# An mLSTM projection that works on the un-normalised residual, with the norm's scale multiplied in where each product leaves PSUM

## The chip, the cores and the metric

One core of one Trainium2 chip runs the whole program in a single launch. The metric is the device time of one execution in microseconds (us). It is called the same within 0.2%, which is 1.6 us here.

## The reference

The reference takes 256 tokens of width 1024, puts 16 learned tokens in front (272 in all) and runs two blocks. What matters for this change is the first:

```
h = h + 0.5 * rmsnorm(swiglu(rmsnorm(h, g0)), g1)      # feed-forward 0, called f0 in the kernel
u = rmsnorm(h, g2)
y = mlstm_mixer(u)                                      # stage a
h = h + rmsnorm(y, g3)
h = h + 0.5 * rmsnorm(swiglu(rmsnorm(h, g4)), g5)      # feed-forward 1, f1

rmsnorm(x, g) = x * rsqrt(mean(x*x) + 1e-6) * g         # mean over the 1024 features of a token

mlstm_mixer(u): z = u @ w_in
    q, k = silu(causal_conv(z[qk columns], 4 taps)); v, og, gates = other columns of z
    lf = log_sigmoid(forget gates);  mLSTM over 8 heads;  y = h_out * sigmoid(og);  return y @ w_out
```

The second block has two layers (l0, l1): modulated norm, projections, attention and a short convolution, an output product and a post-norm added to the residual.

The scale of a norm is one number for each token. A product with weights is linear, so `(h * g2 * r) @ w` equals `r * ((h * g2) @ w)` when r belongs to the token.

## The kernel before

**Layout.** The residual `hT` lies transposed, features on the 128 partitions in 8 tiles of 128, tokens along the free axis (272 in f0 and a, 256 later). Every matrix product runs as three matmuls for each 128x128 weight tile, of the rounded weight `w1` and its remainder `w2` with the rounded activation `u1` and its remainder `u2` (`products`, L309). The weights come as 245 chunks of 128x1024 through five buffers. ScalarE rounds a chunk to `w1` (L739), VectorE makes `w2` (L1033), and five buffers of each are kept (NW = 5). So `split_to(c)` in either engine's program is the order to convert all chunks up to c at that place, and TensorE starts a block of 24 matmuls only when its chunk's `w2` is there.

**Order.** Each engine runs a written list of instructions in order. Engines meet at semaphores only. PSUM banks 0 to 3 are given out in rotation by `place` (L298), which waits until the bank's earlier content is read; banks 4 to 7 are named.

**Between f0 and a.** `normalised` (L1247) on VectorE computes from the column sums of f0's output the scale r1 of its own norm, then from three sums the scale r2 of the next norm (`first_scale` L1191, `second_scale` L1219). GpSimd takes both powers (L1603) and TensorE spreads each over the partitions with transposes (`spread` L369, `both_scales` L494), with `dense` filler matmuls between. Tile by tile VectorE then scales y (L1236), adds it to h for tiles 0 and 4 (GpSimd adds the others, L1609), multiplies h by gain and r2 into `tmp` (L1276), ScalarE rounds it (L841) and VectorE makes the remainder (L1255). TensorE's `head` (L334) takes three chunks at once (gates, qk 0, v 0) tile by tile as u arrives.

**Between a and f1** the kernel already works in the other way (`weighed` L1424): u is h times the gain alone, made before r2 is known. r2 is spread in the middle of the head and copied to `r0`, and the evacuation of the gate product multiplies by `r0`.

**Inside the mLSTM.** For j = 0 to 7 TensorE makes qk block j, v block j and the transposes of v block j-1 (L521). ScalarE's list for each j is: convert chunk A, copy the qk product to `zp` (L857), start the convolution in `cv` with the last tap (L858), convert chunk B, copy v to `vT` (L864), for j = 2 and 3 a part of the logarithm of the forget gate, and the silu of the finished convolution (L874). VectorE's list is: chunk A, three taps (L1346), chunk B, copy the transposed v to `Vs` (L1333), for j = 2, 4 and 5 steps of the gates (`log_gates`). Chunk A of j is chunk 70+2j+1, chunk B 70+2j+2. At j = 7 they are 85 and 86; before that, VectorE and ScalarE convert 70, and 71 to 73 at j = 1.

Then for heads h = 0 to 7: TensorE makes the output-gate block og h+2, transposes y h-1 (L564), sums over the keys (L556), and for each pair of heads makes mask and scores (L536, L545). VectorE adds the mask (L1366), ScalarE takes exponentials (L891), VectorE multiplies by the scores (L1377), makes denominators (L1384 to L1390) and gates the output (L1394), and ScalarE takes the tanh of og from PSUM (L883) and scales the numerators (L899, L900).

**At the end** `token_outputs` (L679) takes all four rotation banks ahead of its first product.

## Time and profile before

| what | us |
|---|---|
| median of 3 runs | 808.71 (808.56 to 810.04) |
| profiled execution, device time | 810.16 |
| its span | 808.2 |
| TensorE busy in the span | 798.9 (99%) |
| VectorE busy | 593.4 (73%) |
| ScalarE busy | 417.0 (52%) |
| GpSimd busy | 145.6 (18%) |
| granted TensorE clock, mean | 0.993 |

A busy share says how much of the span an engine worked, not whether the work was in time. TensorE is nearly always busy, so what counts is each place where it has to wait for the others, and how early the others are elsewhere. The 1.96 us between the span and the device time lie before and after the recorded instructions.

### The profile page before, as it was taken

The page shows a single profiled execution, that of the slowest core. Times are in us where ns is not written, and L with a number is a line of the kernel's source. Part 1 is how long each engine was busy: PE and PEld are TensorE (multiplying, and loading weights), DVE is VectorE, ACT ScalarE, POOL GpSimd, SP SyncE. Part 2 cuts the span into 40 slices and gives each one's busy share as a digit, 9 for nine tenths or more (in the row PEclk, how much of TensorE's full clock was granted, in tenths as well). Part 3 has the DMA queues.
Part 4 walks back from the last instruction along what each step waited for, and adds up shares of the span by engine and source line. Part 5 has one row for each costly group of instructions (what it writes and reads, how often), then busy time and mean ns, then how long its engine had stood idle before and what let it go on. Part 6 is the DMA issues. An engine that isn't in the chain of part 4 may idle for free.

```text
span 808.2 us, 15624 instructions
## 1 busy us (share of the span) xinstructions
PE 798.9 (99%) x6338; PEld 774.1 (96%) x6338; DVE 593.4 (73%) x957; ACT 417.0 (52%) x710; POOL 145.6 (18%) x158
## 2 busy tenths in 40 slices
PE   9999999999999999999999999999999999999997
PEld 9999999999999999999999999999899999899986
DVE  6777777698687986788777779986667567667653
ACT  7544444544367565555444455536655454565541
POOL 3800000041320000020000004240235302035510
PEclk9999999999899999999999999999999999999999
DMA  9876667685336643558777779546544651744531
GB/s 328 307 260 227 237 241 249 205 320 180 118 113 214 191 127 82 179 183 302 272 238 257 252 237 337 167 131 212 161 150 132 181 165 56 268 138 144 148 101 52
DMA packets 45190, 158.83 MB, mean 197 GB/s; under 512 B 5040, under 2 KB 6576, under 8 KB 45120
## 3 DMA queue, kind: packets, MB, share of 16 engines
q1 hardware_dynamic: 45120, 157.85, 58.9%
q8 instruction: 50, 0.82, 0.4%
q14 instruction: 20, 0.16, 0.1%
HBM read 156.76 MB, written 1.06 MB: 195 GB/s over the span
## 4 chain that ended last, share of the span: by engine, by line
PE 96%; DVE 2%; issue 1%; ACT 0%; POOL 0%; DVEq 0%; POOLq 0%
PE ps L312 26%; PE ps L314 25%; PE ps L313 25%; PE ps L664 3%; PE ps L357 2%; PE ps L353 2%; PE ps L354 2%; PE ps L365 1%; PE ps L328 1%; PE ps L556 1%; PE ps L628 1%; PE ps L647 1%; PE ps L637 1%; PE ps L690 1%; PE ps L692 1%
## 5 line engine op out<-in xcount | busy, mean ns | idle before, releaser
L1033 DVE TENSOR_TENSOR w<-raw,w 128x1024 fp32r<-128x1024 f32 x245 | 299.4, 1235 | 135.5 <-ACT w L739 135.1
L312 PE MATMUL ps<-u,w 128*128 128x256 f32 (+1 forms) x1231 | 353.2, 287 | 0.0
L314 PE MATMUL ps<-u,w 128*128 128x256 f32 (+1 forms) x1231 | 349.7, 284 | 0.0
L313 PE MATMUL ps<-u,w 128*128 128x256 f32 (+1 forms) x1231 | 349.0, 284 | 0.0
L739 ACT CAST w<-raw 128x1024 fp32r<-128x1024 f32 x245 | 254.1, 1049 | 124.4 <-PE ps L314 104.7
L312 PEld LDWEIGHTS ps<-u,w 128*128 128x128 f32 x1231 | 232.1, 189 | 6.2 <-issue 4.3
L314 PEld LDWEIGHTS ps<-u,w 128*128 128x128 f32 x1231 | 232.3, 189 | 0.0
L313 PEld LDWEIGHTS ps<-u,w 128*128 128x128 f32 x1231 | 231.6, 188 | 0.0
L312 PE MATMUL ps<-h,w 128*128 128x272 f32 (+1 forms) x352 | 100.3, 285 | 0.0
L314 PE MATMUL ps<-h,w 128*128 128x272 f32 (+1 forms) x352 | 100.0, 284 | 0.0
L313 PE MATMUL ps<-h,w 128*128 128x272 f32 (+1 forms) x352 | 99.8, 284 | 0.0
L1594 POOL TENSOR_TENSOR sqa<-sqa,sq 128x272 f32<-128x272 f32 (+1 forms) x12 | 15.7, 1308 | 311.1 <-ACT sq L804 311.1
L312 PEld LDWEIGHTS ps<-h,w 128*128 128x128 f32 x352 | 66.3, 188 | 0.0
L313 PEld LDWEIGHTS ps<-h,w 128*128 128x128 f32 x352 | 66.2, 188 | 0.0
L314 PEld LDWEIGHTS ps<-h,w 128*128 128x128 f32 x352 | 66.1, 188 | 0.0
L1624 POOL TENSOR_SCALAR Sb<-Sb,st 128x256 f32<-128x256 f32 x32 | 45.2, 1428 | 87.9 <-DVE st L1473 87.9
L1052 DVE SCALAR_TENSOR_TENSOR acc<-adr,cact,acc 128x1024 f32<-128x1024 f32 x42 | 58.2, 1406 | 0.0
L782 ACT ACTIVATE si<-tmp 128x272 f32<-128x272 f32 (+1 forms) x44 | 18.7, 424 | 70.3 <-DVE tmp L1145 70.3
L1150 DVE TENSOR_TENSOR hf<-si,ps 128x272 f32<-128x272 f32 (+1 forms) x44 | 18.9, 429 | 21.2 <-ACT si L782 21.2
L1603 POOL TENSOR_TENSOR rst<-sst,eps 128x2 f32<-128x2 f32 (+1 forms) x4 | 3.0, 748 | 148.8 <-DVE sst L1196 135.5
L353 PE MATMUL ps<-u,w 128*128 128x256 f32 (+1 forms) x105 | 27.2, 290 | 1.2 <-ACT u L926 0.8
L354 PE MATMUL ps<-u,w 128*128 128x256 f32 (+1 forms) x105 | 26.8, 286 | 0.0
(252 smaller groups left out, 1045.2 us busy)
## 6 DMA issues: line engine op xcount, KB each, us to landing
raw<-wst SPq DMA_DIRECT2D x245, 512.0 KB, 4.6
adr<-wada SPq DMA_DIRECT2D x48, 512.0 KB, 3.9
Bt<-bias_rows SPq DMA_DIRECT2D x8, 192.0 KB, 4.0
hT<-xT SPq DMA_DIRECT2D x4, 272.0 KB, 5.2
outT<-yg SPq DMA_DIRECT2D x4, 256.0 KB, 2.0
cs<-cst SPq DMA_DIRECT2D x1, 140.0 KB, 5.1
cs<-cst SPq DMA_DIRECT2D x1, 128.0 KB, 7.0
vc<-vec SPq DMA_DIRECT2D x1, 101.0 KB, 3.5
```

Of the source, the lines that this page charges most:

```text
L312: e.matmul(out, a, x1, start=first, stop=False)
L313: e.matmul(out, a, x2, start=False, stop=False)
L314: return e.matmul(out, b, x1, start=False, stop=last)
L353: e.matmul(ps[:, b, 0:n], w1[:, (c + j) % NW, o:o + P], x1[:, kt, :], start=i == 0, stop=False)
L354: e.matmul(ps[:, b, 0:n], w2[:, (c + j) % NW, o:o + P], x1[:, kt, :], start=False, stop=False)
L664: m = e.matmul(ps[:, b_[tt], :], xx[:, kt, 128 * tt:128 * tt + 128], ww, start=kt == 0 and i == 0, stop=kt == 7 and i == 2)
L739: e.copy(w1[:, k % NW, :], raw[:, k % NRAW, :]).then_inc(*tick(s_upper, k))
L782: e.activation(si[f][:, j % 2, :], zg[:, j % 2, 0:n], ACT.Silu).then_inc(*tick(s_si, (f, j)))
L1033: e.tensor_tensor(w2[:, k % NW, :], raw[:, k % NRAW, :], w1[:, k % NW, :].bitcast(F32), ALU.subtract).then_inc(*tick(s_split, k))
L1052: e.scalar_tensor_tensor(a, w, x, a, ALU.mult, ALU.add).then_inc(*tick(s_acc, k))
L1150: e.tensor_tensor(hf[f][:, i, :], si[f][:, i, :], out_of(ku, n), ALU.mult).then_inc(*reading(ku))
L1624: e.tensor_scalar(Sb[l][:, h % 4, t, :], Sb[l][:, h % 4, t, :], st_[l][:, h % 4, 4 + t:5 + t], None, ALU.mult).then_inc(*tick(s_nrm, (l, h ...
```

## The change

1. **f0 to a** goes the way of a to f1. `weighed` takes the stage as an argument on ScalarE and VectorE, TensorE's `both_scales("f0", T)` is gone, 4 dense matmuls and the spread of r1 stand at the start of its `mlstm`, and the spread of r2 is a hook in the middle of the head. u is h times gain 2.
2. **r2 at the evacuations.** VectorE multiplies each qk product (8 of 128x272), the two gate products (8x272) and each og product (8 of 128x256) by `r0` on the way out of PSUM. ScalarE's copy to `zp` is gone; its first tap and its tanh read SBUF now, after VectorE. `v` is scaled after its transposes: `r0` is transposed once (3 transposes on TensorE, two small copies to `rv` on VectorE), and ScalarE copies V to `Vs` with three multiplies by a column of `rv` for each head, where VectorE copied it with two copies.
3. **Fewer norm steps**, at every boundary: the sums are read from PSUM by `tensor_scalar` with two column operands, without the copies and the separate add.
4. **Last banks one by one**: `token_outputs` takes a bank ahead of the first product that writes it.
5. GpSimd adds h tile 2 between the two powers in f0 too, and leaves tile 1 to VectorE. Its clears of `Vs` and `SW` wait for the spread of r1 in place of that of r2, and for the clear of `zp`, which VectorE now does after it has copied `r0`. One more memset (`msq`) stands at the start.

```diff
             def mlstm():                                             # TensorE
+                dense(4)
+                e.wait_ge(s_pow.handle, at(s_pow, ("r1", "f0")))
+                spread(("r1", "f0"), 6, T, rst)
+                def spread_scale(i):
+                    if i == KT // 2:
+                        e.wait_ge(s_pow.handle, at(s_pow, ("r2", "f0")))
+                        spread(("r2", "f0"), 5, T, rst2)
+                def scale_columns():
+                    b = place(("rv",), 6)
+                    e.wait_ge(*read(("r2", "f0")))
+                    for j, (a, z) in enumerate(tok_tiles(T)):
+                        m = e.transpose(ps[0:z - a, b, 128 * j:128 * j + 128], r0[:, a:z], ident)
+                    m.then_inc(*tick(s_rvtr, 0))
...
-                head(keys[:3], c, x1, x2, T, *u_of("a"))
+                head(keys[:3], c, x1, x2, T, *u_of("a"), hook=spread_scale)
                 for j in range(8):
                     if j:
                         block(("qk", j), c + 1 + 2 * j, x1, x2, T)
+                        if j == 1:
+                            scale_columns()
...
             def token_outputs():
-                b_ = [[place(("tok", t, hf)) for hf in range(2)] for t in range(2)]
...
-                        out = ps[:, b_[t][hf], :]
+                        out = ps[:, place(("tok", t, hf)) if i == 0 else bank_of(("tok", t, hf)), :]
...
             ffn_out(0, "f0", T)
-            both_scales("f0", T)
             mlstm()
...
             def mlstm():                                             # ScalarE
-                e.wait_ge(s_zero.handle, 1)
+                def v_scaled(h):
+                    b = bank_of(("vt", h))
+                    e.wait_ge(s_vtr.handle, at(s_vtr, h))
+                    if h == 0:
+                        e.wait_ge(s_pad.handle, at(s_pad, "last"))
+                        e.wait_ge(*read(("rv",)))
+                    for j, n in enumerate((P, P, NMETA)):
+                        m = e.mul(Vs[0:n, j, h, 0:128], ps[0:n, b, 128 * j:128 * j + 128], rv[0:n, j:j + 1])
+                    m.then_inc(*reading(("vt", h)))
                 split_to(c + NW - 1)
                 for j in range(8):
                     if j:
                         split_to(c + 1 + 2 * j + NW - 1)
-                    proj(("qk", j))
-                    if j > 1:
-                        e.wait_ge(s_cv.handle, at(s_cv, (j - 2, 2)))
-                    e.copy(zp[:, i, 3:3 + T], out_of(("qk", j), T)).then_inc(*tick(s_zp, j))
-                    e.mul(cv[:, i, :], out_of(("qk", j), T), a_tap(3, j)).then_inc(*reading(("qk", j)))
+                    e.wait_ge(*read(("qk", j)))
+                    e.mul(cv[:, i, :], zp[:, i, 3:3 + T], a_tap(3, j)).then_inc(*tick(s_cvm, j))
                     if j:
                         split_to(c + 2 + 2 * j + NW - 1)
                     proj(("v", j))
...
                     e.copy(vT[:, i, :], out_of(("v", j), T)).then_inc(*reading(("v", j)))
+                    if j:
+                        v_scaled(j - 1)
...
                 def gate_block(h):
                     split_to(c + 17 + h + NW - 1)
-                    proj(("og", h))
-                    e.activation(og[:, h, :], out_of(("og", h)), ACT.Tanh, scale=0.5).then_inc(*reading(("og", h)))
+                    e.wait_ge(*read(("og", h)))
+                    e.activation(og[:, h, :], og[:, h, :], ACT.Tanh, scale=0.5).then_inc(*tick(s_tanh, ("og", h)))
...
                 gate_block(1)
+                v_scaled(7)
...
             def first_scale(s, n, eps_of):                           # VectorE: sst, then
+                e.reciprocal(inv[:, 0:len(tt)], sst[:, 0:len(tt)]).then_inc(*tick(s_stat, ("inv", s)))
+                e.wait_ge(s_stat.handle, at(s_stat, ("inv", s)))
+                for j, (a, z) in enumerate(tt):
+                    m = e.tensor_scalar(msq[0:z - a, j:j + 1], ps[0:z - a, 7, 2 * j + 1:2 * j + 2], inv[0:z - a, j:j + 1],
+                                        msh[0:z - a, j:j + 1], ALU.mult, ALU.add)
...
             def second_scale(s, n):
+                for j, (a, z) in enumerate(tt):
+                    m = e.tensor_scalar(msq[0:z - a, j:j + 1], ps[0:z - a, 5, j:j + 1], rst[0:z - a, j:j + 1],
+                                        msq[0:z - a, j:j + 1], ALU.mult, ALU.add)
+                e.tensor_scalar(msh[:, 0:len(tt)], msq[:, 0:len(tt)], EPS, None, ALU.max).then_inc(*tick(s_stat, ("max", s)))
...
             def mlstm():                                             # VectorE
-                e.wait_ge(s_spread.handle, at(s_spread, ("r2", "f0")))
                 e.memset(zp[:, :, 0:3], 0.0).then_inc(*tick(s_zero, 0))
-                split_to(c + NW - 1)
                 proj(("gates",))
+                e.wait_ge(*read(("r2", "f0")))
-                e.tensor_scalar(gi, ps[0:8, b, 0:T], vc[0:8, V_GB:V_GB + 1], None, ALU.add).then_inc(*tick(s_gate, "i"))
-                e.tensor_copy(fx_, ps[32:40, b, 0:T]).then_inc(*reading(("gates",)))
+                e.tensor_tensor(gi, ps[0:8, b, 0:T], r0[0:8, :], ALU.mult).then_inc(*tick(s_gate, "zi"))
+                e.tensor_tensor(fx_, ps[32:40, b, 0:T], r0[32:40, :], ALU.mult).then_inc(*reading(("gates",)))
+                e.wait_ge(s_gate.handle, at(s_gate, "zi"))
+                e.tensor_scalar(gi, gi, vc[0:8, V_GB:V_GB + 1], None, ALU.add).then_inc(*tick(s_gate, "i"))
...
                 for j in range(8):
                     if j:
                         split_to(c + 1 + 2 * j + NW - 1)
-                    e.wait_ge(s_zp.handle, at(s_zp, j))
+                    proj(("qk", j))
+                    if j > 1:
+                        e.wait_ge(s_cv.handle, at(s_cv, (j - 2, 2)))
+                    e.tensor_tensor(zp[:, i, 3:3 + T], out_of(("qk", j), T), r0, ALU.mult).then_inc(*reading(("qk", j)))
+                    if j == 1:
+                        e.wait_ge(s_rvtr.handle, 1)
+                        e.tensor_copy(rv[:, 0:2], ps[:, 6, 0:256:128])
+                        e.tensor_copy(rv[0:16, 2:3], ps[0:16, 6, 256:257]).then_inc(*reading(("rv",)))
                     for tap in range(3):
                         if tap == 0:
-                            e.wait_ge(*read(("qk", j)))
+                            e.wait_ge(s_cvm.handle, at(s_cvm, j))
...
                     if j:
                         split_to(c + 2 + 2 * j + NW - 1)
-                        v_copied(j - 1)
...
+                def gate_scaled(h):
+                    proj(("og", h))
+                    e.tensor_tensor(og[:, h, :], out_of(("og", h)), r0[:, 16:T], ALU.mult).then_inc(*reading(("og", h)))
                 split_to(c + 17 + NW - 1)
+                gate_scaled(0)
                 weights(0)
                 weighted(0)
                 split_to(c + 18 + NW - 1)
-                v_copied(7)
+                gate_scaled(1)
                 for h in range(NH):
                     if h < NH - 2:
                         split_to(c + 19 + h + NW - 1)
+                        gate_scaled(h + 2)
...
-            normalised("f0", "a", T, lambda k: norm_gain(2, k), None, eps0)
+            weighed("f0", "a", T, 2, C_A, eps0)
```

In `weighed` VectorE's list is that of a to f1: first scale; tile by tile scaled y, h added (tiles 0, 1, 4), the remainder of u; the second scale after tile 1; then chunk C_A + 4 = 70 and the copy to `r0`.

## Rows read from the trace of the kernel before

**Rows 1.** The page's chain that ended last, share of the span by engine.
```profile
PE 96%; DVE 2%; issue 1%; ACT 0%; POOL 0%; DVEq 0%; POOLq 0%
```
**Rows 2.** Windows: length, busy us of PE, PEld, DVE, ACT, POOL; clock; DMA; GB/s.
```profile
213.80:220.60 6.80, 6.80 (x31) 6.04 (x31) 5.25 (x16) 1.26 (x3) 3.31 (x5) 0.50 0.10 34
```
**Rows 3.** Timeline of PE, f0 to a: start, us, instruction, [idle before <- releaser].
```profile
214.94 1.65 PE L328 MATMUL ps<-dz 128*128 128x256 f32 x6
...
218.61 0.43 PE L353 MATMUL ps<-u,w 128*128 128x272 f32 x1
```
**Rows 4.** Timeline of DVE: chunks 79, 81 and 83, and the first pair's weights.
```profile
255.79 1.23 DVE L1033 TENSOR_TENSOR w<-raw,w 128x1024 fp32r<-128x1024 f32 x1 [3.85 <-ACT w L739]
256.93 1.57 DVE L1346 SCALAR_TENSOR_TENSOR cv<-zp,vc,cv 128x272 f32<-128x272 f32 x3
...
262.68 1.19 DVE L1033 TENSOR_TENSOR w<-raw,w 128x1024 fp32r<-128x1024 f32 x1
...
269.74 1.21 DVE L1033 TENSOR_TENSOR w<-raw,w 128x1024 fp32r<-128x1024 f32 x1
...
280.88 1.33 DVE L1366 TENSOR_TENSOR SW<-ps,cs 128x256 f32<-128x256 f32 x6
282.73 1.53 DVE L1377 SCALAR_TENSOR_TENSOR SW<-ps,SW 128x256 f32<-128x256 f32 x6 [0.53 <-ACT SW L891]
```
**Rows 5.** Timeline of PE: sums over the keys of heads 0, 2 and 4.
```profile
285.06 1.28 PE L556 MATMUL ps<-Vs,SW 128*128 128x129 f32 x10
...
294.85 1.28 PE L556 MATMUL ps<-Vs,SW 128*128 128x129 f32 x10
...
304.63 1.28 PE L556 MATMUL ps<-Vs,SW 128*128 128x129 f32 x10
```
**Rows 6.** Timeline of DVE: mask added for pairs 1, 2 and 3.
```profile
287.76 1.31 DVE L1366 TENSOR_TENSOR SW<-ps,cs 128x256 f32<-128x256 f32 x6
...
297.28 1.33 DVE L1366 TENSOR_TENSOR SW<-ps,cs 128x256 f32<-128x256 f32 x6
...
307.16 1.33 DVE L1366 TENSOR_TENSOR SW<-ps,cs 128x256 f32<-128x256 f32 x6
```
**Rows 7.** Timeline of PE: last matmul before, first matmul of the token outputs.
```profile
777.59 0.28 PE L314 MATMUL ps<-u,w 128*128 128x256 f32 x1
...
779.17 0.47 PE L690 MATMUL ps<-w,m 128*128 128x512 f32 x1 [1.31 <-DVE cw L1521]
```
**Rows 8.** Timeline of DVE and ACT, a to f1.
```profile
343.11 0.42 DVE L1236 TENSOR_TENSOR yg<-yg,ps 128x256 f32<-128x256 f32 x1 [0.65 <-PE ps L372]
...
353.03 0.51 ACT L926 ACTIVATE u<-hT,vc 128x256 fp32r<-128x256 f32 x1 [1.17 <-POOL hT L1609]
```
**Rows 9.** Timeline of ACT in the mLSTM, the part of j = 3.
```profile
246.49 1.03 ACT L739 CAST w<-raw 128x1024 fp32r<-128x1024 f32 x1
...
247.71 0.48 ACT L858 ACTIVATE cv<-ps,vc 128x272 f32<-128x272 f32 x1
248.09 1.04 ACT L739 CAST w<-raw 128x1024 fp32r<-128x1024 f32 x1
249.03 0.37 ACT L864 COPY vT<-ps 128x272 f32<-128x272 f32 x1
249.42 1.28 ACT L870 ACT_TABLE_LOAD   x1
...
254.29 0.53 ACT L874 ACTIVATE qk<-cv,vc 128x272 f32<-128x272 f32 x1
254.72 1.03 ACT L739 CAST w<-raw 128x1024 fp32r<-128x1024 f32 x1
```
**Rows 10.** Timeline of ACT: numerators of head 1 scaled.
```profile
293.42 0.37 ACT L899 ACTIVATE ytm<-ps,den 128x128 f32<-128x128 f32 x1
293.68 0.36 ACT L900 ACTIVATE ytm<-ps,den 128x128 f32<-128x128 f32 x1
```
**Rows 11.** Timeline of POOL, l0 to l1: the second power.
```profile
671.17 0.71 POOL L1603 TENSOR_TENSOR rst<-msh,eps 128x2 f32<-128x2 f32 x1 [0.72 <-DVE msh L1233]
```

More of the change, by code:

```diff
@@ L1191, in first_scale @@
             def first_scale(s, n, eps_of):
-                nt = len(sum_tiles(n))
+                tt = sum_tiles(n)
                 e.wait_ge(s_colsum.handle, at(s_colsum, ("sum", s) if s[0] == "f" else ("sq", s, 7)))
                 if eps_of is None:
-                    e.tensor_scalar(sst[:, 0:2], ps[:, 7, 0:4:2], EPS, None, ALU.add).then_inc(*tick(s_stat, ("sst", s)))
+                    m = e.tensor_scalar(sst[:, 0:2], ps[:, 7, 0:4:2], EPS, None, ALU.add)
                 else:
                     m = e.tensor_tensor(sst[:, 0:2], ps[:, 7, 0:4:2], eps_of[:, 0:2], ALU.add)
-                    if nt == 3:
+                    if n == T:
@@ L1216, in first_scale @@
-                e.wait_ge(s_stat.handle, at(s_stat, ("quot", s)))
-                e.tensor_tensor(msh[:, 0:nt], msh[:, 0:nt], inv[:, 0:nt], ALU.add).then_inc(*tick(s_stat, ("msh", s)))
-            def second_scale(s, n):
-                nt = len(sum_tiles(n))
-                e.wait_ge(s_stat.handle, at(s_stat, ("msh", s)))
-                e.wait_ge(s_pow.handle, at(s_pow, ("r1", s)))
-                if nt == 3:
-                    e.wait_ge(*read(("sumc", s)))
-                    e.tensor_tensor(inv[:, 0:nt], sums[:, 6:9], rst[:, 0:nt], ALU.mult).then_inc(*tick(s_stat, ("mix", s)))
-                    e.wait_ge(s_stat.handle, at(s_stat, ("mix", s)))
-                else:
-                    e.wait_ge(s_colsum.handle, at(s_colsum, ("sumc", s)))
-                    e.tensor_tensor(inv[:, 0:nt], ps[:, 5, 0:2], rst[:, 0:nt], ALU.mult).then_inc(*reading(("sumc", s)))
-                    e.wait_ge(*read(("sumc", s)))
-                e.tensor_tensor(msh[:, 0:nt], msh[:, 0:nt], inv[:, 0:nt], ALU.add).then_inc(*tick(s_stat, ("add", s)))
-                e.wait_ge(s_stat.handle, at(s_stat, ("add", s)))
-                e.tensor_scalar(msh[:, 0:nt], msh[:, 0:nt], EPS, None, ALU.max).then_inc(*tick(s_stat, ("max", s)))
@@ L1422, in mlstm, with weighed @@
                 mixer_out("a", c + 25)
-            def weighed():
-                first_scale("a", S, None)
-                e.wait_ge(s_spread.handle, at(s_spread, ("r1", "a")))
-                e.wait_ge(*read(("out", "a", KT - 1)))
+            def weighed(s, nxt, n, g, c, eps_of):
+                first_scale(s, n, eps_of)
+                e.wait_ge(s_spread.handle, at(s_spread, ("r1", s)))
+                e.wait_ge(*read(("out", s, KT - 1)))
                 for k in range(-1, KT):
                     if k < KT - 1:
-                        scaled("a", k + 1, S)
+                        scaled(s, k + 1, n)
@@ L1443, in weighed @@
-                split_to(C_F[1] + NW - 1)
-                e.wait_ge(s_spread.handle, at(s_spread, ("r2", "a")))
-                e.tensor_copy(r0[:, 0:S], ps[:, 5, 0:S]).then_inc(*reading(("r2", "a")))
+                        second_scale(s, n)
+                        if s == "a":
+                            e.wait_ge(s_stat.handle, at(s_stat, ("max", "a")))
+                            e.tensor_scalar(eps0[:, 0:2], msh[:, 0:2], EPS, None, ALU.mult).then_inc(
+                                *tick(s_stat, ("eps", "a")))
@@ L1447, in attention @@
+                split_to(c + NW - 1)
+                e.wait_ge(s_spread.handle, at(s_spread, ("r2", s)))
+                if s == "a":
+                    e.wait_ge(*read(("og", NH - 1)))
+                e.tensor_copy(r0[:, 0:n], ps[:, 5, 0:n]).then_inc(*reading(("r2", s)))
             def attention(l):
@@ L1569, in first_input @@
                 e.memset(sst[:, :], 1.0).then_inc(*tick(s_one, "sst"))
+                e.memset(msq[:, :], 1.0).then_inc(*tick(s_one, "msq"))
                 e.wait_ge(s_one.handle, at(s_one, "sst"))
@@ L1611, in boundary @@
             def boundary(s, n):
-                nt = len(sum_tiles(n))
-                e.wait_ge(s_stat.handle, at(s_stat, ("sst", s)))
-                power(rst, sst, nt, ("r1", s))
-                e.wait_ge(s_stat.handle, at(s_stat, ("max", s)))
-                power(rst2, msh, nt, ("r2", s))
+                first_power(s, n)
+                second_power(s, n)
                 h_added(s, n, (1, 2, 3, 5, 6, 7))
```

82 lines of the change are left out of this document (39 added, 43 removed).

## The prediction

> **What bounds the kernel now.** I read the page's chain first, then the granted clock around the change, then each engine's timeline there, and asked at each place how early the other engines are. The chain is 96% TensorE [rows 1], so a gain must come from a place where TensorE waits or runs slowly, and a loss from an engine that is only just in time now. There are three such places.
>
> At f0 to a the array ran at half its clock (0.50 of 2.4 GHz, so the 1.2 GHz level) for 6.8 us [rows 2], after 24 matmuls of one or two columns, and six filler matmuls took 1.65 us there [rows 3]. The head began at 218.61 [rows 3]. The reader is to see that this stretch is short work at a low clock, where the order of the norm steps decides.
>
> In the mLSTM TensorE has no wait at all, but VectorE and ScalarE are hardly ahead of it. The mask of the first pair of heads is added at 280.88, the products with the scores end at 284.26 (282.73 + 1.53) [rows 4], and TensorE starts the sums that need them at 285.06 [rows 5]: 0.8 us of slack. Later the mask steps are 9.52 and 9.88 us apart [rows 6], where TensorE's sums are 9.79 and 9.78 apart [rows 5]. So the loop of VectorE and ScalarE is as long as TensorE's own. That the waits of TensorE are zero hides this.
>
> At the token outputs TensorE waits 1.31 us for a bank [rows 7].
>
> **The change part by part.** I sum against the profiled execution (span 808.2, 810.16 with what lies around it). It lies 1.45 above the median of 808.71, so the difference is applied to the median.
>
> *f0 to a, the start.* The first spread ends at about 215.0, just ahead of the fillers [rows 3]. Four fillers now stand ahead of it: 4 x 0.24 (1.65 less the overlap of the last, over 6) [rows 3] = 1.0, so it ends at 216.0. From the first scaled tile to the start of the last u the same code takes 9.92 us between a and f1 (343.11 to 353.03) and the last u takes 0.51 [rows 8]. I add 0.2 for 272 columns in place of 256 and take off 0.3 for the norm steps that are gone: the last u is there at 216.0 + 10.3 = 226.3. The first u comes 1.6 after the first scaled tile, so the head starts at 217.6, 1.0 earlier than 218.61 [rows 3], and it is no longer short of u tiles, which I put at 0.2 more. Extra on TensorE are the 3 transposes of the scale, 0.3. So TensorE gains 0.9 here, with bounds of 0.3 less (the fillers cost what they cost) and 1.4 more (the clock back at 217 and not at 220.6).
>
> *The chain of VectorE and ScalarE, entering the mLSTM.* It does not gain as much. From 226.3: cast of chunk 70 1.03, its remainder 1.23, the copy to r0 0.35, the gates' two products and bias 1.1, the product into zp 0.43 (as the scaling of y [rows 8]), first tap 0.5, three taps 1.57 [rows 4], silu 0.43. The waits between engines (0.04 each) and the overlap of successive instructions cancel to 0.1. The cast of chunk 71 then starts at 233.0, 0.4 earlier than before.
>
> *The loop over j.* Here the order changes. Before, ScalarE went cast A, zp, first tap, cast B, v, silu, while VectorE made the remainder of A: nothing that ScalarE did waited for VectorE but the silu. Now ScalarE's first tap waits until VectorE has made the remainder of A and then zp. ScalarE's round is cast A 1.03 [rows 9], wait for the remainder 1.18 (255.79 to 256.93, plus 0.04) [rows 4], wait for zp 0.47, first tap 0.39 (247.71 to 248.09), cast B 0.94 (248.09 to 249.03), v 0.28, three scalings of V 0.78, silu 0.43 (254.29 to 254.72) [rows 9]: 5.5 us, against 4.3 before (remainder A 1.14, taps 1.48, remainder B 1.14, V copies 0.53, all VectorE). The three scalings are priced by the numerators, 0.26 from start to start for 128x128 [rows 10]; their bounds are 0 (hidden beside the taps) and 1.1 (3 x 0.37). TensorE's round is 6.4, so the longer round alone would be covered. But two things take the cover: ScalarE's logarithm at j = 3 with three table loads (249.42 to 254.29) [rows 9], which stands behind the scalings, and VectorE's gate steps at j = 4 and 5, with which it was busy without a gap from 255.79 on (6.89 to chunk 81, 7.06 to chunk 83) [rows 4].
>
> Lateness of VectorE against before, chunk by chunk: -0.4 at 71. Chunk 75 +0.9: in j = 1 ScalarE has the scalings (0.8) and the taps stand behind zp (0.5). Chunk 77 +1.3. Chunk 79 +3.4: j = 3 waits for remainder and zp (1.6 less the 0.3 of the old copy) and has the scalings (0.8) ahead of the table loads. Then VectorE's own round is the bound: it gains zp and the wait for the first tap (1.0) and loses the V copies (0.5), +0.5 at each j, so chunk 81 +3.9 and 83 +4.4. At j = 6 and 7 ScalarE's 5.5 is the bound against 4.3: chunk 85 +5.6, 87 +6.8. The og product adds 0.35 ahead of the first mask: +7.2, at 288.1. The pair's products then end 3.38 later (280.88 to 284.26) [rows 4], at 291.5, and TensorE's sums start there and not at 285.06 [rows 5]: +6.4. On the way TensorE waits at the transposes of v 4 to 7 and for og 0, but these waits lie inside the 6.4.
>
> *The loop over heads.* First pair to second: 6.88 before (280.88 to 287.76) [rows 4, 6]. Now two og products (0.7), and head 7's scalings and the tanh stand ahead of a cast, where the V copies stood beside it: 9.3, +2.4, so the second mask is 9.6 late. After that each pair has two og products more on a loop that is serial through both engines (mask, exponentials, cast, remainder, og product, output, denominator, numerators, cast, and again): +0.65 for each of two pairs against 9.52 and 9.88 [rows 6], 10.3 and 10.9 late, and og 7 makes 11.2. At 10.5 a pair the loop is longer than TensorE's 9.78 [rows 5], so TensorE waits. It had about 1.0 of slack to the last outputs. So it enters a's output product 10.2 late. This holds the gain at f0 to a, which is lost: TensorE's early start only lengthens its wait.
>
> Bounds of this term: 6.4 if the loop over heads is hidden, 12 if the scalings cost 1.1 and every handover 0.1. The nearest rows give 10.2.
>
> *The end.* The bank of the first token product was read long before, that of the fourth is needed nine matmuls later. 779.17 - 777.59 - 0.12 of a normal step = 1.46 [rows 7], all of it gained, since TensorE alone is the bound to the end.
>
> *Fewer norm steps.* Into l0 and f1 a filler or the head covers them: nothing. Into l1 the second power starts at 671.17, 0.72 after GpSimd was free [rows 11], and one step of 0.1 less lies ahead of it: 0.1 gained, between 0 and 0.3. The extra memset and the moved clears cost nothing: the first V copy comes several us after them.
>
> *Sum.* +10.2 - 1.46 - 0.1 = +8.6; 808.7 + 8.6 = 817.3.
>
> **The rivals.** *All hidden, faster.* TensorE stays the bound through the mLSTM. For it speaks that TensorE shows no wait there and that its round over j, 6.4 us, is longer than ScalarE's new one; against it the 0.8 us of slack [rows 4, 5]. -0.9 - 1.46 - 0.1 = -2.5: 806.2, and 804.8 with the clock back sooner.
>
> *Only the loop over j costs.* The loop over heads catches up, if handovers there are shorter than I read. Against it are the 9.88 [rows 6]. +6.4 - 1.6 = +4.8: 813.5.
>
> *The clock falls in the new waits.* TensorE would wait some 1 to 2.5 us at six or more places, and it lost its clock at f0 to a after about 2.5 us of tiny matmuls [rows 2]. A stretch like that at half clock does 3.4 us less work, one of half its length 1.7. Where TensorE waits anyway it is free, so I count one such stretch that lies behind the loops or at their tight end: +1.7 to +3.4, 819 to 820.7. The Trainium skill (TensorE: Matmul & The Clock Gate, the section on HAM oscillation) says that waits between bursts of matmuls can put the array back to half its clock again and again. By that rule this rival is the likelier. The trace has the low level once more only, after f1, and not at a or l0, where waits of 0.2 to 0.8 us stand beside the sums, so I leave it behind the forecast.
>
> *The steps aren't fewer in time.* A `tensor_scalar` with two column operands may take longer than the copies: some 0.3 us at most at l1, in no way decisive.
>
> **How the numbers follow.** Forecast 0.59, 817.3, its own range 814.5 to 820. Loop over j only 0.13, 813.5. Clock 0.12, 820. All hidden 0.12, 806.2. The rest, 0.04, no change. The range 812.5 to 821 leaves out the hidden case and little else. What can be told from no change is 0.2%, 1.6 us: faster 0.13, same 0.03, slower 0.84.
>
> **What would show it.** Head of a starting about 1 us earlier; chunk 79's remainder near 259, chunk 87's near 286.6 and the first mask near 288; TensorE waiting for vT and later for the numerators and SW, some 10 us in all; mask steps 10.2 to 10.5 apart; no wait at L690. I am wrong if TensorE's waits between 228 and 322 stay under 2 us. Then the round of ScalarE is shorter than I add it up. A clock under 1.00 in the mLSTM would show the third rival.

## The result and the profile after

| what | before | after |
|---|---|---|
| median | 809.34 (4 runs beside those of after) | 821.55 (820.13 to 821.87, 4 runs) |
| ratio to before | | 1.0148, 95% interval 1.0132 to 1.0164 |
| profiled execution, its span | 810.16, 808.2 | 821.64, 819.6 |
| mean granted TensorE clock | 0.993 | 0.986 |

The changed kernel is slower by 12.2 us, 1.5%. The forecast was 817.3 with 812.5 to 821.0; the median lies 0.55 above the range.

The page's chain of after answers to [rows 1]:

```profile
PE 84%; DVE 7%; ACT 6%; issue 3%; POOL 1%; DVEq 0%; POOLq 0%; ACTq 0%
```

TensorE's share of the chain fell from 96% to 84%: 13% of it now runs through VectorE and ScalarE. TensorE's waits by releaser (us in total, times, longest) say where:

```profile
PE ps L543 <- ACT vT L889: 2.4, 2, 1.9
PE ps L582 <- ACT ytm L927: 2.2, 3, 1.5
PE ps L574 <- DVE SW L1394: 1.8, 1, 1.8
...
PE ps L314 <- DVE w L1061: 1.0, 1, 1.0
```

All four are in the mLSTM, where there was no wait before. They add up to 7.4 us. The wait for the token bank [rows 7] is gone: the first token product is L708 and starts without one.

```profile
790.66 0.40 PE L708 MATMUL ps<-w,m 128*128 128x512 f32 x1
```

VectorE as the mLSTM begins, from the copy of the scale to the first taps (timeline: start, us, instruction, [idle before <- releaser]):

```profile
228.49 0.43 DVE L1472 COPY tmp<-ps 128x272 f32<-128x272 f32 x1
...
229.03 0.43 DVE L1308 TENSOR_TENSOR g<-ps,tmp 8x272 f32<-8x272 f32 x1
229.49 0.43 DVE L1309 TENSOR_TENSOR g<-ps,tmp 8x272 f32<-8x272 f32 x1
229.96 0.64 DVE L1311 TENSOR_SCALAR g<-g,vc 8x272 f32<-8x272 f32 x1
230.63 0.44 DVE L1352 TENSOR_TENSOR zp<-ps,tmp 128x272 f32<-128x272 f32 x1
231.73 1.58 DVE L1364 SCALAR_TENSOR_TENSOR cv<-zp,vc,cv 128x272 f32<-128x272 f32 x3 [0.66 <-ACT cv L883]
```

The three gate steps stand in line ahead of zp and take 1.60 us (229.03 to 230.63). Then the round of j = 4 on VectorE, and the landmarks that answer to [rows 4, 6]:

```profile
260.09 1.23 DVE L1061 TENSOR_TENSOR w<-raw,w 128x1024 fp32r<-128x1024 f32 x1 [5.61 <-ACT w L756]
261.23 0.43 DVE L1352 TENSOR_TENSOR zp<-ps,tmp 128x272 f32<-128x272 f32 x1
262.25 1.58 DVE L1364 SCALAR_TENSOR_TENSOR cv<-zp,vc,cv 128x272 f32<-128x272 f32 x3 [0.59 <-ACT cv L883]
...
267.48 1.19 DVE L1061 TENSOR_TENSOR w<-raw,w 128x1024 fp32r<-128x1024 f32 x1
...
288.98 1.32 DVE L1383 TENSOR_TENSOR SW<-ps,cs 128x256 f32<-128x256 f32 x6
290.83 1.53 DVE L1394 SCALAR_TENSOR_TENSOR SW<-ps,SW 128x256 f32<-128x256 f32 x6 [0.53 <-ACT SW L918]
...
298.25 1.31 DVE L1383 TENSOR_TENSOR SW<-ps,cs 128x256 f32<-128x256 f32 x6
...
308.44 1.33 DVE L1383 TENSOR_TENSOR SW<-ps,cs 128x256 f32<-128x256 f32 x6
```

VectorE does zp, then idles 0.59 us until ScalarE has made the first tap from it. ScalarE on its side idles for zp: 1.64 us at j = 2, 3, 4 and 7, and 3.5 and 3.7 at j = 5 and 6, where VectorE has gate steps first. At j = 3:

```profile
248.53 1.03 ACT L756 CAST w<-raw 128x1024 fp32r<-128x1024 f32 x1
251.20 0.52 ACT L883 ACTIVATE cv<-zp,vc 128x272 f32<-128x272 f32 x1 [1.64 <-DVE zp L1352]
251.63 1.04 ACT L756 CAST w<-raw 128x1024 fp32r<-128x1024 f32 x1
252.58 0.37 ACT L889 COPY vT<-ps 128x272 f32<-128x272 f32 x1
252.85 0.85 ACT L874 ACTIVATE Vs<-ps,rv 128x128 f32<-128x128 f32 x3
253.72 1.28 ACT L897 ACT_TABLE_LOAD   x1
```

Each engine waits for the other once in a round, so the round is the sum of both parts. TensorE's sums over the keys of head 0 answer to [rows 5]:

```profile
291.59 2.29 PE L574 MATMUL ps<-Vs,SW 128*128 128x129 f32 x10 [1.84 <-DVE SW L1394]
```

Lateness of after against before, at the same instruction in both profiles, beside the forecast:

| point | before | after | late | forecast |
|---|---|---|---|---|
| VectorE, remainder of chunk 71 | 234.41 | 234.84 | +0.4 | -0.4 |
| chunk 79 | 255.79 | 260.09 | +4.3 | +3.4 |
| chunk 87 | 279.73 | 287.50 | +7.8 | +6.8 |
| first mask | 280.88 | 288.98 | +8.1 | +7.2 |
| masks of pairs 1, 2, 3 | | | +10.5, +11.2, +11.8 | +9.6, +10.3, +10.9 |
| TensorE, first low products of a's output | 314.33 | 325.44 | +11.1 | +10.2 |
| f1's head, second low products | 347.07 | 358.77 | +11.7 | +10.2 |
| f1's column sums | 528.12 | 540.31 | +12.2 | +10.2 |
| l0's column sums | 668.20 | 681.00 | +12.8 | +10.2 |
| l1's head, second low products | 675.95 | 688.81 | +12.9 | +10.1 |
| first token product | 779.17 | 790.66 | +11.5 | +8.6 |

Two things stand in it. From chunk 71 on to a's output the lateness runs parallel to the forecast, 0.8 to 1.0 above it. And behind a it grows by another 1.8 us, where the forecast had nothing. The experiments take these in turn.

One thing the table hides. The two executions were not level ahead of the change: TensorE reaches f0's last column sums at 211.39 in before and at 210.94 in after. Counted from there, after is 0.45 later at every point than the table says, so 1.3 above the forecast at chunk 71 and not 0.8.

### The profile page after: what moved, and what is told of

It is laid out like the page before. It is cut to its first block, busy times and chain, and to the rows that moved or that the text cites. A ratio compares the mean times of both kernels' runs of the same rounds, so it can differ in the third digit from the quotient of the medians.

```text
span 819.6 us, 15624 instructions
## 1 busy us (share of the span) xinstructions
PE 804.7 (98%) x6339; PEld 778.6 (95%) x6339; DVE 593.9 (72%) x949; ACT 422.1 (51%) x726; POOL 145.1 (18%) x158
## 3 DMA queue, kind: packets, MB, share of 16 engines
HBM read 156.76 MB, written 1.06 MB: 193 GB/s over the span
## 4 chain that ended last, share of the span: by engine, by line
PE 84%; DVE 7%; ACT 6%; issue 3%; POOL 1%; DVEq 0%; POOLq 0%; ACTq 0%
PE ps L314 23%; PE ps L316 22%; PE ps L315 22%; PE ps L684 3%; DVE w L1061 2%; ACT w L756 2%; PE ps L355 2%; PE ps L356 2%; PE ps L359 2%; PE ps L367 2%; PE ps L330 1%; PE ps L648 1%; PE ps L667 1%; ACT SW L918 1%; PE ps L657 1%
## 5 line engine op out<-in xcount | busy, mean ns | idle before, releaser
L314 PE MATMUL ps<-u,w 128*128 128x256 f32 (+1 forms) x1231 | 354.1, 288 | 1.0 <-DVE w L1061 1.0
L314 PEld LDWEIGHTS ps<-u,w 128*128 128x128 f32 x1231 | 232.9, 189 | 7.5 <-issue 4.3
L314 PE MATMUL ps<-h,w 128*128 128x272 f32 (+1 forms) x352 | 100.5, 286 | 0.0
L314 PEld LDWEIGHTS ps<-h,w 128*128 128x128 f32 x352 | 66.3, 188 | 0.0
```

The costliest lines, as they stand in the source:

```text
L314: e.matmul(out, a, x1, start=first, stop=False)
```

## Experiments

Ratios are to the kernel before, in runs on the same chip (its medians there: 809.89 for the first four, 810.03 for the next four, 810.29 for the two after, 809.58 for the last two).

### Which evacuation costs: one scale at a time

The changed kernel with q and k, V and the output gates left unscaled (b1_none), and with one of the three scaled (b2_qk, b3_v, b4_og); where it isn't scaled, the order of before stands on both engines. The scale is left out there, so none of the four computes the whole reference. The excerpts below are from ScalarE's list, the last one from VectorE's, where b1_none copies V.

```diff
-                    e.wait_ge(*read(("qk", j)))
-                    e.mul(cv[:, i, :], zp[:, i, 3:3 + T], a_tap(3, j)).then_inc(*tick(s_cvm, j))
+                    proj(("qk", j))
+                    if j > 1:
+                        e.wait_ge(s_cv.handle, at(s_cv, (j - 2, 2)))
+                    e.copy(zp[:, i, 3:3 + T], out_of(("qk", j), T)).then_inc(*tick(s_cvm, j))
+                    e.mul(cv[:, i, :], out_of(("qk", j), T), a_tap(3, j)).then_inc(*reading(("qk", j)))
...
-                    if j:
-                        v_scaled(j - 1)
...
-                    e.wait_ge(*read(("og", h)))
-                    e.activation(og[:, h, :], og[:, h, :], ACT.Tanh, scale=0.5).then_inc(*tick(s_tanh, ("og", h)))
+                    proj(("og", h))
+                    e.activation(og[:, h, :], out_of(("og", h)), ACT.Tanh, scale=0.5).then_inc(*reading(("og", h)))
...
+                        v_copied(j - 1)
```

> The changed kernel, but the qk, v and og products leave PSUM unscaled, by the instructions and in the order of the kernel before (so q, k, v and og lack the norm's scale; the gates have it). It keeps the new boundary f0 to a, the fewer norm steps and the banks one by one. My theory (the chain of VectorE and ScalarE in the mLSTM is what costs, and only the evacuations put it there): no wait of TensorE between 228 and 322 us, 2 to 3 us faster than before. Rival (the cost is at the boundary: the fillers, the low clock, the late r0): still 8 us or more slower than before. Rival (half and half): within 2 us of before.

> As b1_none, but with the scale in the qk evacuations: VectorE makes zp and ScalarE's first tap waits for it. v and og are unscaled. My theory: the round over j grows from 4.3 to 5.1 us, chunk 79 is some 2.5 us late, the first mask some 5 to 6.5 late, so 2 to 4 us slower than before. Rival (the three scalings of V make the round long, zp is hidden): faster than before by 1 to 2.5 us.

> As b1_none, but with the scale in the copies of V (three multiplies on ScalarE for each head; scale transposed on TensorE). qk and og are unscaled. My theory: alone they fit in ScalarE's waits for the taps, only j = 3 and head 7 pay, 1 to 2.5 us faster than before. Rival (ScalarE's extra 0.8 us a head is the cost): 3 us or more slower than before.

> As b1_none, but with the scale in the og evacuations: VectorE multiplies, ScalarE's tanh waits for it. qk and v are unscaled. My theory: each pair of heads is 0.65 us longer, on a loop that had about 1 us of slack in all: mask steps 10.2 and 10.5 us apart, within 1.5 us of before. Rival (the loop over heads was only long because it was entered late): mask steps stay at 9.5 and 9.9, 2 to 3 us faster than before.

| kernel | median | ratio | interval | first mask | steps between masks |
|---|---|---|---|---|---|
| b1_none | 808.44 | 0.9978 | 0.9969 to 0.9988 | 279.75 | 6.88, 9.52, 9.89 |
| b2_qk | 817.02 | 1.0081 | 1.0066 to 1.0096 | 288.69 | 6.87, 9.53, 9.89 |
| b3_v | 807.98 | 0.9974 | 0.9964 to 0.9983 | 279.89 | 7.19, 9.53, 9.87 |
| b4_og | 812.15 | 1.0027 | 1.0018 to 1.0037 | 280.21 | 9.06, 10.18, 10.53 |

Over b1_none, q and k cost 8.6 us, the output gates 3.7, V nothing; together 11.8, against 13.0 to 13.8 for the whole change over b1_none by the ratios. The masks name the mechanisms. The product into zp makes the first mask 8.9 us later and leaves the steps as they were. The og products leave the first mask and make all steps longer, by 2.2, 0.7 and 0.6. The steps agree with the forecast for og (+2.4 and +0.65 twice), but the time does not agree with what I expected of b4_og: within 1.5 us of before, and it is 2.2 slower by its ratio. For V theory and size agree (three scalings cost 0.76 each round on ScalarE, which had that much room). b1_none was to be 2 to 3 us faster than before and is 1.8. Of q and k alone I had expected 2 to 4 us more than before; it came to 6.6, and is most of the loss. In each round VectorE has zp (0.43) more and idles 0.59 until the tap is there, and in this kernel it keeps the V copies (0.5) that the whole change takes off it.

### The banks of the token outputs alone

```diff
-                b_ = [[place(("tok", t, hf)) for hf in range(2)] for t in range(2)]
...
-                        out = ps[:, b_[t][hf], :]
+                        out = ps[:, place(("tok", t, hf)) if i == 0 else bank_of(("tok", t, hf)), :]
```

> The kernel before with one part of the change alone: the banks of the token outputs are taken one by one. Theory: the 1.46 us at the first token product are gained and nothing else moves, 1.2 to 1.7 us faster than before, no wait at L690. Rival (the wait is handed on to the next bank or to m2): within 0.5 us of before.

807.23, ratio 0.9975 (0.9955 to 0.9995). From l1's second low products to the first token product it takes 101.72 us, 103.22 before: 1.50 gained, the forecast's 1.46. Of the kernels that compute the whole reference it has the lowest ratio, though the intervals of e1_pad and f3_all below touch its own. (Its profiled span, 805.0, is 3.2 us shorter than that of before. The other 1.7 don't come from the banks: it reaches f0's column sums 0.55 earlier, and takes 0.6 less from them to the end of a's head, with a shorter stretch of low clock, and 0.5 less at l0's head, where it has none.)

### The same change in another order

f1_zp puts VectorE's product into zp ahead of the remainder of the chunk:

```diff
-                    if j:
-                        split_to(c + 1 + 2 * j + NW - 1)
                     proj(("qk", j))
...
                     e.tensor_tensor(zp[:, i, 3:3 + T], out_of(("qk", j), T), r0, ALU.mult).then_inc(*reading(("qk", j)))
+                    if j:
+                        split_to(c + 1 + 2 * j + NW - 1)
```

> The changed kernel with one move: in each j VectorE makes the product into zp ahead of the remainder of chunk A, not behind it. Theory (ScalarE's first tap and VectorE's taps wait for each other there, 1.0 us a round): the first mask comes about 5 to 6 us earlier than in the changed kernel (282 to 284 against 288.98), the loop over heads keeps its cost, 2 to 4 us slower than before. Rival (the added work as such costs, VectorE and ScalarE are full): within 2 us of the changed kernel, 10 or more slower than before.

f2_zp_og, on top of it, issues the og product behind the masks of the next pair (even heads) or behind the denominators (odd heads), and ScalarE's tanh a round later, behind the next cast. VectorE's list, then ScalarE's:

```diff
-                        gate_scaled(h + 2)
                     if 0 < h < NH - 2:
                         output(h - 1)
                     denominators(h)
                     if h % 2 == 0 and h < NH - 2:
                         weights(h // 2 + 1)
+                        gate_scaled(h + 2)
                         weighted(h // 2 + 1)
+                    elif h < NH - 2:
+                        gate_scaled(h + 2)
...
                     if h < NH - 2:
-                        gate_block(h + 2)
+                        split_to(c + 19 + h + NW - 1)
+                    if h < NH - 1:
+                        gate_tanh(h + 1)
```

> As f1_zp, and in the loop over heads the og product of VectorE stands where it waited for ScalarE (behind the denominators of odd heads, between the two steps of the weights of even heads), and ScalarE's tanh comes one round later, behind a cast; head 7's scalings of V stand ahead of that cast. Theory: mask steps back at 9.6 to 9.9 us, 2 us or more faster than f1_zp, between 2 us faster and 1 slower than before. Rival (this loop is bound by the sum of work): no faster than f1_zp.

f3_all, on top of that, makes zp of block 0 before the gates' products:

```diff
+                proj(("qk", 0))
+                e.wait_ge(*read(("r2", "f0")))
+                e.tensor_tensor(zp[:, 0, 3:3 + T], out_of(("qk", 0), T), r0, ALU.mult).then_inc(*reading(("qk", 0)))
                 proj(("gates",))
-                e.wait_ge(*read(("r2", "f0")))
```

> As f2_zp_og, and VectorE makes zp of block 0 ahead of the two gate products. Theory: the chain enters the loop over j up to 1 us earlier, 0.2 to 1 us faster than f2_zp_og, 0.5 to 2.5 faster than before. Rival (TensorE is the bound again in f2_zp_og already): the same as f2_zp_og.

| kernel | median | ratio | interval | first mask | steps |
|---|---|---|---|---|---|
| f1_zp | 814.22 | 1.0051 | 1.0036 to 1.0066 | 282.54 | 9.28, 10.19, 10.55 |
| f2_zp_og | 810.76 | 1.0013 | 1.0002 to 1.0024 | 280.81 | 6.93, 9.52, 10.14 |
| f3_all | 809.55 | 0.9994 | 0.9984 to 1.0003 | 280.99 | 6.92, 9.52, 10.13 |

The order alone brings the changed kernel back to the time of the kernel before: 7 us with zp early, 3 with the og products off the chain, and 1.2 by the medians (1.5 by the ratios) with the entry. The profiles show 0.7 of the last step: TensorE's wait for the remainder of chunk 71 is 0.97 us in f2_zp_og and 0.23 in f3_all. The first mask is no earlier there, since f3_all's profile ran at the low clock for longer at f0 to a (213.7 to 220.5, against 215.3 to 218.7). VectorE's round in f1_zp shows no idle time ahead of the taps any more:

```profile
257.51 1.23 DVE L1061 TENSOR_TENSOR w<-raw,w 128x1024 fp32r<-128x1024 f32 x1 [3.78 <-ACT w L756]
258.65 1.57 DVE L1364 SCALAR_TENSOR_TENSOR cv<-zp,vc,cv 128x272 f32<-128x272 f32 x3
260.13 1.22 DVE L1061 TENSOR_TENSOR w<-raw,w 128x1024 fp32r<-128x1024 f32 x1
```

So nearly all of the loss is the place of the products in two engines' lists, not their work. What is left is about 1.3 us: f3_all has 0.9994, b1_none, with the same boundaries and banks but no scaling of q, k, V and og, 0.9978, and their intervals only just overlap. In f3_all's mLSTM TensorE still waits twice, and the last mask step is 10.13 against 9.89:

```profile
235.65 0.39 PE L314 MATMUL ps<-u,w 128*128 128x272 f32 x1 [0.23 <-DVE w L1063]
...
314.12 0.35 PE L355 MATMUL ps<-y,w 128*128 128x256 f32 x1 [0.56 <-DVE og L1429]
```

Even in this order the change brings nothing over the banks alone (0.9975).

### The low clock in the new waits

After's profile has the low level (0.50) behind two of the new waits and at the start of f1. Windows of after (length, busy PE, PEld, DVE, ACT, POOL; clock; DMA share; GB/s):

```profile
260.00:264.00 4.00, 2.08 (x17) 1.85 (x16) 3.25 (x6) 2.36 (x7) 0.00 (x0) 1.00 0.37 108
264.00:268.00 4.00, 4.00 (x22) 4.00 (x21) 3.89 (x7) 1.54 (x3) 0.00 (x0) 0.57 0.64 201
...
291.00:295.50 4.50, 3.91 (x20) 3.48 (x20) 2.80 (x8) 2.87 (x9) 0.00 (x0) 0.62 0.32 95
...
352.00:358.00 6.00, 5.71 (x34) 5.42 (x35) 4.66 (x16) 1.59 (x5) 1.64 (x3) 0.72 0.38 108
```

That is the third rival's sign. d1_keep puts filler matmuls into the three longest waits, into the bank that is placed there anyway (`keep(b, n)` issues n of 128x256; ahead of the transposes of v 3, the sums over the keys of head 0, the output of head 1):

```diff
+                    b = place(("vt", h), None if h >= NH - 2 else 4 + h % 2)
+                    if h == 3:
+                        keep(b, 15)
                     e.wait_ge(*read(("v", h)))
-                    b = place(("vt", h), None if h >= NH - 2 else 4 + h % 2)
...
+                    if h == 0:
+                        b = place(("num", h))
+                        keep(b, 15)
                     e.wait_ge(*read(("score", h)))
...
+                    b = place(("y", h), 6)
+                    if h == 1:
+                        keep(b, 12)
                     e.wait_ge(*read(("num", h)))
-                    b = place(("y", h), 6)
```

> The changed kernel with filler matmuls (128x256, results overwritten) in TensorE's three longest new waits of the mLSTM: 15 ahead of the transposes of v 3 (it waits 1.9 us there), 15 ahead of the sums over the keys of head 0 (1.8), 12 ahead of the output of head 1 (1.5), each a little shorter than the wait. Theory A, the two stretches at half clock behind these waits (264.4 to 267.8 and 291.6 to 295.0) are absorbed, since VectorE and ScalarE set the order there: the clock in the mLSTM goes to 1.00, first mask at 289, mask steps 9.3, 10.2 and 10.5 as before, and the time stays within 0.7 us of the changed kernel without fillers. Theory B, the low clock there is part of the excess over the forecast: 1.7 us less for one stretch, 3.4 for both, that is 818 to 820.

> The changed kernel once more, for the comparison with the fillers on the same chip: 820 to 822, 1.013 to 1.017 of the kernel before. If the low stretches differ from those of its first profile (0.50 at 213.4 to 220.2, then 264.4 to 267.8, 291.6 to 295.0, and half the clock lost behind f1 and l0), the two profiles together show what such a stretch costs where it comes and where it does not.

d1_keep: 821.27, 1.0136 (1.0119 to 1.0153). The changed kernel again: 821.61, 1.0139 (1.0124 to 1.0155). In d1_keep the clock stays at its 2.4 GHz level through the mLSTM, and the masks stand where they stood:

```profile
260.00:264.00 4.00, 3.81 (x31) 3.60 (x30) 3.34 (x6) 2.70 (x7) 0.00 (x0) 1.00 0.53 148
264.00:268.00 4.00, 4.00 (x34) 4.00 (x33) 3.89 (x7) 1.15 (x2) 0.00 (x0) 1.00 0.53 164
...
291.00:295.50 4.50, 4.44 (x40) 3.84 (x40) 2.42 (x7) 2.87 (x8) 0.00 (x0) 1.00 0.29 74
```

```profile
288.58 1.32 DVE L1395 TENSOR_TENSOR SW<-ps,cs 128x256 f32<-128x256 f32 x6
...
297.87 1.31 DVE L1395 TENSOR_TENSOR SW<-ps,cs 128x256 f32<-128x256 f32 x6
```

Steps 9.29, 10.19 and 10.54, as in after. The clock did fall there, and it cost nothing: TensorE had to wait for VectorE at the next stop in any case. From f0's column sums to a's first low output products it is 114.50 us in after, 114.26 in the second profile of after and 114.51 in d1_keep.

Nor does such a wait always bring the low clock. The second profile of after has the same two waits:

```profile
264.26 0.55 PE L543 MATMUL ps<-cs,vT 128*128 128x128 f32 x3 [1.90 <-ACT vT L889]
...
292.37 1.65 PE L574 MATMUL ps<-Vs,SW 128*128 128x129 f32 x10 [1.80 <-DVE SW L1394]
```

Behind the first the granted clock stays at 1.00, behind the second it is 0.50 from 293.3 to 300.2. f1_zp and b4_og, with waits up to 1.5 us, have no low stretch there. Behind a the low clock costs a little. The column sums of a to f1's second low products take 6.70 us in before and 6.71 in the second profile of after, both at full clock, and 7.35 in the first profile, with the low stretch: 0.65. The same from l0 to l1 is 7.81 at full clock and 8.64 in the second profile, which has its low stretch there. The two profiles of after have their low stretches at different boundaries (the first at f1 and l0, the second at l1), and their spans, 819.6 and 820.1, are close.

### The missing microsecond: where the operands lie

Stage lengths on TensorE fall into two groups: before and a1_banks on one side, every kernel made from the changed one on the other. Within a group f1 is the same to 0.01 us (181.05; 181.53 to 181.54), l0 to 0.2 (127.41 to 127.44; 127.78 to 127.98). The changed one allocates two small buffers, msq and rv, 16 bytes a partition each, in the middle of the list, and all buffers behind them move by 16 to 32 bytes. e1_pad is a1_banks with such a gap and no other difference; e2_place is the changed kernel without it.

The gap of e1_pad, on a1_banks:

```diff
         msh = sb("msh", [P, 4])
+        pad1 = sb("pad1", [P, 4])
         rst2 = sb("rst2", [P, 4])
+        pad2 = sb("pad2", [P, 4])
```

e2_place, on the changed kernel, whose sums buffer has these columns free (its memset is narrowed to columns 0 to 7):

```diff
-        msq = sb("msq", [P, 4])
+        msq = sums[:, 8:12]
...
-        rv = sb("rv", [P, 4])
+        rv = sums[:, 4:8]
```

> The kernel before with the token banks one by one, and two unused buffers of 16 bytes a partition where the change allocates msq and rv, so that every buffer behind them lies where it lies in the changed kernel; no instruction differs. Stage lengths by TensorE in the profiles so far are the same to 0.02 us in each group of kernels and differ between the groups with and without the change's two buffers: f1 from its second low product to the column sums 181.05 without, 181.54 with; l0 likewise 127.4 without, 127.8 with; a's output product with its sums 26.04 without, 25.71 with; from l1's head to the first token product 101.72 without, 101.85 with. Theory A, where the operands lie sets this: 181.54, 127.8, 25.7 and 101.85 here, 0.6 to 0.8 us in all, so 807.8 to 808.2. Theory B, it is the fewer norm steps or their instructions: all four as without the change, and 807.2.

> The changed kernel with msq and rv laid into columns of the sums buffer that it no longer uses, so that every later buffer lies where it lies in the kernel before; the instructions are the same. Theory A (place of the operands): f1 181.05 in place of 181.54, l0 127.4 in place of 127.8, head of l1 to first token product 101.72; 0.6 to 0.9 us faster than the changed kernel, 820.5 to 821.0. Theory B: no stage changes, 821.5.

| stage on TensorE | before | a1_banks | e1_pad | after | e2_place |
|---|---|---|---|---|---|
| a, first low output products to column sums | 26.04 | 26.04 | 25.71 | (waits) | (waits) |
| f1, second low products to column sums | 181.05 | 181.05 | 181.54 | 181.54 | 181.05 |
| l0, the same | 127.44 | 127.41 | 127.80 | 127.79 | 127.31 |
| l1's second low products to first token product | 103.22 | 101.72 | 101.86 | 101.85 | 101.73 |

The ends of the f1 stage and of the l0 stage in a1_banks, and in e1_pad:

```profile
345.95 0.63 PE L357 MATMUL ps<-u,w 128*128 128x256 f32 x4
...
527.00 0.50 PE L365 MATMUL ps<-wts,sqa 128*128 128x1 f32 x4
...
539.14 0.63 PE L357 MATMUL ps<-u,w 128*128 128x256 f32 x4
...
666.55 0.50 PE L365 MATMUL ps<-wts,sqa 128*128 128x1 f32 x4
```

```profile
346.25 0.63 PE L359 MATMUL ps<-u,w 128*128 128x256 f32 x4
...
527.79 0.50 PE L367 MATMUL ps<-wts,sqa 128*128 128x1 f32 x4
...
540.65 0.63 PE L359 MATMUL ps<-u,w 128*128 128x256 f32 x4
...
668.45 0.50 PE L367 MATMUL ps<-wts,sqa 128*128 128x1 f32 x4
```

All stages went where theory A put them. In time e1_pad took 809.27, 0.9993 (0.9984 to 1.0002), against a1_banks' 0.9975, and e2_place 819.57, 1.0132 (1.0117 to 1.0148), against 1.0139 and 1.0148 for the changed kernel. Both medians missed what I expected (807.8 to 808.2; 820.5 to 821.0). The intervals overlap, so by time alone neither is shown; the stage lengths show it, 1.0 us in f1, l0 and l1 together, less 0.33 at a. Where it comes from is seen in l0's output product, nine matmuls of the same shapes in both (a row x3 stands for three). First before, then after:

```profile
645.34 0.52 PE L357 MATMUL ps<-m,w 128*128 128x256 f32 x3
...
646.40 0.52 PE L357 MATMUL ps<-m,w 128*128 128x256 f32 x3
```

```profile
657.72 0.52 PE L359 MATMUL ps<-m,w 128*128 128x256 f32 x3
...
658.80 0.52 PE L359 MATMUL ps<-m,w 128*128 128x256 f32 x3
```

Nine such matmuls take 1.08 us in after and in e1_pad, 1.06 in before, a1_banks and e2_place, some 2 ns more for each. At a it is the other way round (1.08 in a1_banks, 1.06 in b1_none and e1_pad). Which property of the address it is was not tried.

## Why the prediction fell short

*The mechanism and its place: right.* First tap behind zp, V scalings, table loads, then VectorE's own round, then the og products. The increments agree: chunk 79 to 87 grew by 3.5 us against 3.4 forecast, the mask steps were 9.27, 10.19 and 10.54 against 9.3, 10.2 and 10.5. The waits that were named came, at L543, L574 and L582, though 6.4 us of them (7.4 with the one at L314, which was not named) and not 10. Most of the rest of the 11.1 us of lateness lies in the two stretches at 0.50 behind them, 3.4 us each, in which TensorE did half the work.

*The step that failed first: the entry.* "The gates' two products and bias 1.1" took 1.60: 0.43, 0.43 and 0.64 with no overlap, where neighbours in the loop overlap by 0.1. The first tap after zp took 0.66 and not 0.5, and from the copy to r0 to the first gate product it is 0.54 (228.49 to 229.03) and not 0.35, with the clear of zp in between. So chunk 71 was 0.8 later than forecast, and since VectorE and ScalarE set the pace from there on, all that follows was as well. f3_all, which makes zp ahead of the gate steps, took 0.7 us off TensorE's wait for chunk 71 and 1.2 to 1.5 off the time.

*A second miss at the entry, covered by luck.* The forecast took 0.3 off for the norm steps that are gone and added 0.2 for the wider tiles, which makes 9.8 from the first scaled tile to the last u on ScalarE. It took 10.34 (215.52 to 225.86). Between a and f1 the same steps went from 9.92 to 9.84, so fewer steps save 0.1 and, as far as these rows tell, the wider tiles cost 0.5. The last u was still there at 226.4, near the 226.3 of the forecast, only because this execution was 0.45 ahead at f0's column sums.

*A reading that was wrong and didn't show.* I gave TensorE 0.8 us of slack before the sums, counting from the end of all six products. The sums of head 0 need only its own three: in after they start 0.76 after the products begin (290.83 to 291.59), and so in before the slack was about 1.6. With a mask 0.9 later than forecast, the sums came at +6.5 against +6.4. Two errors cancelled there, but not at the outputs behind.

*The rest of the miss lies behind a, where the forecast had one term of -0.1.* Lateness grows by 0.65 for the low clock at f1, 0.49 in f1 and 0.35 in l0 with the place of the operands, 0.26 at l0's boundary (low clock in both profiles, a little worse here). The fewer norm steps, forecast to gain 0.1 into l1, gave nothing: l0's column sums to l1's second low products take 7.81 in after and 7.75 in before.

*The end: right.* 1.37 gained with the 0.13 that the operands take there, 1.50 in a1_banks; forecast 1.46.

*f0 to a: right in size, and lost as forecast.* From f0's column sums to the last tile of a's head TensorE took 17.12 us in before and 16.12 in after, 1.0 less (forecast 0.9). It took 16.53 in a1_banks and 15.86 in b1_none, 0.7 less with stretches at low clock of about the same length, yet both have the first mask at 279.75.

*The third rival* came in its sign and in part in its price: 0.65 us where the low stretch fell on f1's head, nothing in the loops. By the Trainium skill (TensorE: Matmul & The Clock Gate, HAM oscillation) waits between bursts can lower the clock again and again. The traces agree in part: it fell behind the waits of 1.9 and 1.8 us in the first profile of after, and only behind that of 1.8 in the second.

*From spans to medians.* The median is 4.2 us above the forecast of 817.3. Of that, 2.8 are the misses named here: the sum was made between profiled spans, +8.6 forecast and +11.4 measured. The rest is the step from one execution to the median. 808.71 + 11.4 would be 820.1, inside the range; but the kernel before has 809.34 in the comparison, 0.6 more, and its profiled execution lay 0.8 above that median, that of after 0.1.

## What to carry to other kernels

When a product moves to where its operand leaves PSUM, look not at its price but at who waits for it: put it first in its engine's list, ahead of work that isn't awaited. A stage that is 99% TensorE can have two other engines just behind it, so add up the round of those engines across each handover before moving work onto them. And keep a small new buffer from shifting the large ones: allocate it last, or compare stage lengths against a version with only the gap. Before reading lateness between two profiles, level them at a point ahead of the change.

## What the runs showed of the hardware

- Moving all later buffers by 16 to 32 bytes a partition changed the spacing of 128x256 matmuls by about 2 ns (1.06 to 1.08 us for nine), in either direction by stage: +0.49 us in f1, +0.39 in l0, -0.33 at a's output.
- Stage lengths without a wait repeat well between kernels and executions, so that they resolve what medians with intervals of 0.2 to 0.4% can't: f1 took 181.05 in three kernels and 181.53 or 181.54 in ten, l0 127.31 to 127.44 and 127.78 to 127.98.
- The granted clock fell to 0.50 after waits of 1.9 and 1.8 us within a stage of dense matmuls, but not after the same 1.9 us wait in another execution of the same kernel, and the place of the low stretches behind the loops changed as well.
- An exchange between VectorE and ScalarE cost 0.03 to 0.04 us beside the instructions: VectorE's idle time of 0.59 is the tap's 0.52 and two handovers. The exchange also gives up the overlap of neighbours in one list: in f1_zp the taps start 1.14 us after a remainder that takes 1.23 (257.51 to 258.65), while in after they start 1.02 after zp, which takes 0.43 (261.23 to 262.25).
